# Mixture-of-experts stage: the products of two experts taken one after the other, with a semaphore for each expert's weights

## The reference

```python
def expert_block(args):
    xr, e = args
    return (jax.nn.silu(xr @ w_gate[e]) * (xr @ w_up[e])) @ w_down[e]
...
yb = lax.map(expert_block, (xb, blk_e)).reshape(cap, d)
return jnp.zeros_like(h).at[tok_buf].add(yb * w_buf[:, None])
```

## Time and profile before

| | us |
|---|---|
| median of 3 runs | 2017.88 (2017.27 to 2020.76) |
| profiled execution, its own time | 2020.66 |
| span of its profile | 2018.3 |
| PE busy | 1781.8 (88%), 7064 instructions |
| DVE, ACT, POOL busy | 729.9, 449.8, 397.5 |
| expert stage, first PE row to the last down products | 1475.67 to 1982.97 |
| mean granted TensorE clock | 0.955 |

### The profile page before, as it was taken

One profiled execution on the slowest core, in us unless ns is written; L12 is line 12 of the kernel. 1 busy time (PEld: TensorE's weight loads), 2 busy tenths in 40 slices (PEclk: granted clock), 3 DMA queues, 4 the chain that ended last, 5 costly groups with the idle time before them and its releaser, 6 DMA issues.

```text
span 2018.3 us, 18573 instructions
## 1 busy us (share of the span) xinstructions
PE 1781.8 (88%) x7064; PEld 963.0 (48%) x7064; DVE 729.9 (36%) x1148; ACT 449.8 (22%) x716; POOL 397.5 (20%) x464
## 2 busy tenths in 40 slices
PE   6899999999996999999999999998478878777782
PEld 1455555555554777677765444443423323333330
DVE  1534635455345665556665322124400000000003
ACT  2231231413224443434443000002110000000001
POOL 0103223141317443354441000000010000000000
PEclk9999999999998999999999999999589989899996
DMA  7212321322320111111132725212679999999993
GB/s 278 81 34 78 122 56 45 112 57 68 94 63 22 52 42 42 52 39 44 42 104 87 257 94 187 94 60 89 264 289 428 431 429 430 430 429 429 430 404 153
DMA packets 153554, 350.25 MB, mean 174 GB/s; under 512 B 14065, under 2 KB 104394, under 8 KB 140442
## 3 DMA queue, kind: packets, MB, share of 16 engines
q1 hardware_dynamic: 135962, 325.34, 42.8%
q10 hardware_dynamic: 12496, 15.75, 2.3%
q0 software_dynamic: 5040, 8.40, 1.1%
HBM read 346.09 MB, written 13.32 MB: 178 GB/s over the span
## 4 chain that ended last, share of the span: by engine, by line
PE 71%; DMA 19%; DVE 4%; POOL 3%; issue 2%; ACT 1%; SPq 0%; ACTq 0%; POOLq 0%; DVEq 0%
PE bank L498 10%; PE bank L709 10%; PE bank L747 6%; PE bank L2186 5%; PE bank L1702 5%; PE bank L1279 4%; PE bank L503 4%; DMA arena<-in_w_up_dram 3%; DMA stay<-in_w_up_dram 3%; DMA stay<-in_w_gate_dram 3%; PE bank L1704 3%; PE bank L1721 3%; PE bank L2204 3%; PE bank L494 3%; PE bank L1315 2%
## 5 line engine op out<-in xcount | busy, mean ns | idle before, releaser
L709 PE MATMUL bank<-stay,arena 128*128 128x512 f32 (+1 forms) x704 | 242.7, 501 | 9.9 <-DVE arena L934 7.7
L2186 PE MATMUL bank<-arena 128*64 128x512 f32 x832 | 201.3, 640 | 51.2 <-DMA arena<-in_w_up_dram 35.1
L709 PEld LDWEIGHTS bank<-stay,arena 128*128 128x128 f32 x704 | 133.5, 192 | 111.4 <-issue 101.3
L498 PE MATMUL bank<-arena 128*128 128x512 f32 x384 | 169.0, 593 | 1.5 <-ACT stay L610 1.5
L2186 PEld LDWEIGHTS bank<-arena 128*64 128x64 f32 x832 | 70.9, 147 | 180.1 <-issue 178.5
L2248 DVE TENSOR_TENSOR arena<-arena,bank 128x512 f32<-128x512 f32 x17 | 11.7, 688 | 325.8 <-PE bank L2186 325.8
L747 PE MATMUL bank<-arena,stay 128*128 128x512 f32 x256 | 114.0, 596 | 1.4 <-DVE arena L973 1.4
L1158 POOL TENSOR_TENSOR arena<-arena 128x256 f32<-128x256 f32 x112 | 86.6, 773 | 131.7 <-DVE arena L1472 117.5
L498 PEld LDWEIGHTS bank<-arena 128*128 128x128 f32 x384 | 71.7, 190 | 85.4 <-issue 85.4
L1471 DVE TENSOR_TENSOR arena<-arena 128x256 f32<-128x256 f32 x112 | 63.5, 607 | 132.0 <-ACT arena L1214 100.6
L2101 POOL DMA_INDIRECT y_dram<-arena x17 | 17.1, 1008 | 445.1 <-DVE arena L2255 444.5
(11 more groups left out here) (372 smaller groups left out, 2678.4 us busy)
## 6 DMA issues: line engine op xcount, KB each, us to landing
arena<-in_w_gate_dram SPq DMA_DIRECT2D x26, 2048.0 KB, 25.5
arena<-in_w_up_dram SPq DMA_DIRECT2D x26, 2048.0 KB, 26.9
arena<-in_w_down_dram SPq DMA_DIRECT2D x24, 2048.0 KB, 27.5
arena<-in_w_in_dram SPq DMA_DIRECT2D x58, 512.0 KB, 3.9
arena<-in_w_ada_dram SPq DMA_DIRECT2D x12, 2048.0 KB, 10.9
stay<-in_w_down_dram SPq DMA_DIRECT2D x10, 2048.0 KB, 26.0
stay<-in_w_gate_dram SPq DMA_DIRECT2D x8, 2048.0 KB, 25.7
stay<-in_w_up_dram SPq DMA_DIRECT2D x8, 2048.0 KB, 28.2
```

The lines of the kernel that those rows point to most:

```text
L498: mm = pe.matmul(b[:, :], w[:, k, :], src[:, k, 0:LAT], start=(k == 0), stop=(k == KT - 1))
L709: mm = pe.matmul(ps[:, 0:n], w[:, k, :], hT[:, k, o:o + n], start=(k == 0), stop=(k == KT - 1))
L2186: mm = pe.matmul(b[cols, :], xgT[r][:, k, cols], w[u][:, k, :], start=(k == 0), stop=(k == KT - 1))
```

## The change

The four semaphores `s_w` take only the loads of the first expert, and four other semaphores, which earlier stages had used (`s_x`, `s_ctx`, `s_wdt`, `s_ysum`, standing at 16, 16, 16 and 8), take the loads of the second. PE waits for the first expert's load, does all of its products of the group (16 instructions), waits for the second's and does all of its products. In `down` both output halves of the first expert come ahead of those of the second. What is computed, the loads, their order and the buffers are the same.

```diff
+        s_w_second = [s_x, s_ctx, s_wdt, s_ysum]
+        SECOND = [16, 16, 16, 8]
...
         def landed(chunk):
-            return 32 * (chunk // 4 + 1)
+            return 16 * (chunk // 4 + 1)
...
-                for u in range(2):
-                    sp.dma_start(weights_of(chunk)[u], expert_source(kind, pair[u])).then_inc(s_w[chunk % 4], 16)
+                sp.dma_start(weights_of(chunk)[0], expert_source(kind, pair[0])).then_inc(s_w[chunk % 4], 16)
+                sp.dma_start(weights_of(chunk)[1], expert_source(kind, pair[1])).then_inc(s_w_second[chunk % 4], 16)
...
             def up(chunk, r, loaded, b, done):
                 w = weights_of(chunk)
-                pe.wait_ge(s_w[chunk % 4], loaded)
-                for k in range(KT):
-                    for u in range(2):
-                        cols = slice(u * SLOT, (u + 1) * SLOT)
+                for u in range(2):
+                    if u:
+                        pe.wait_ge(s_w_second[chunk % 4], loaded + SECOND[chunk % 4])
+                    else:
+                        pe.wait_ge(s_w[chunk % 4], loaded)
+                    cols = slice(u * SLOT, (u + 1) * SLOT)
+                    for k in range(KT):
                         mm = pe.matmul(b[cols, :], xgT[r][:, k, cols], w[u][:, k, :], start=(k == 0), stop=(k == KT - 1))
                 mm.then_inc(done, 1)
...
             def down(chunk, loaded, done):
                 w = weights_of(chunk)
                 pe.wait_ge(s_guc, done + 1)
-                pe.wait_ge(s_w[chunk % 4], loaded)
-                for hf in range(2):
-                    for f in range(FT):
-                        for u in range(2):
-                            cols = slice(u * SLOT, (u + 1) * SLOT)
+                for u in range(2):
+                    if u:
+                        pe.wait_ge(s_w_second[chunk % 4], loaded + SECOND[chunk % 4])
+                    else:
+                        pe.wait_ge(s_w[chunk % 4], loaded)
+                    cols = slice(u * SLOT, (u + 1) * SLOT)
+                    for hf in range(2):
+                        for f in range(FT):
                             mm = pe.matmul(bank[5 + hf][cols, :], guT[:, f, cols], w[u][:, f, hf * 512:(hf + 1) * 512],
                                            start=(f == 0), stop=(f == FT - 1))
                 mm.then_inc(s_d, 1)
...
-                up(OVER, 0, landed(OVER) + i * 32, bank[2], s_g)
+                up(OVER, 0, landed(OVER) + i * 16, bank[2], s_g)
```

More of the change, by code:

```diff
@@ L2231, in experts_tensor @@
                 pe.wait_ge(s_sig, PAIRS + i)
-                up(OVER, 0, landed(OVER) + i * 32, bank[2], s_g)
+                up(OVER, 0, landed(OVER) + i * 16, bank[2], s_g)
                 pe.wait_ge(s_gu, PAIRS + i)
-                up(OVER + 1, 0, landed(OVER + 1) + i * 32, bank[3], s_u)
+                up(OVER + 1, 0, landed(OVER + 1) + i * 16, bank[3], s_u)
                 pe.wait_ge(s_guc, PAIRS + i)
@@ L2237, in experts_tensor @@
                 pe.wait_ge(s_yb, PAIRS + i)
-                down(OVER + 2, landed(OVER + 2) + i * 32, PAIRS + i)
+                down(OVER + 2, landed(OVER + 2) + i * 16, PAIRS + i)
         ylc = arena[:, 0:4096].rearrange("p (j d) -> p j d", d=D)
```

## The result

| | before | after |
|---|---|---|
| median of the runs, us | 2019.32 (2017.27 to 2021.93) | 2132.8 (2131.09 to 2134.19) |
| span of the profile, us | 2018.3 | 2129.6 |
| PE busy, us | 1781.8 | 1962.8 |
| mean granted TensorE clock | 0.955 | 0.97 |

The changed kernel is slower: ratio 1.0561, 95% interval 1.0543 to 1.0579, four runs of each in turn. Forecast were 2127.5 us, 2085 to 2203.

The account below looks back on a forecast made before the run. The weight-load queue bounds the expert stage at 30.75 us a block; the new order makes PE the bound at 35.63 us. Over fifteen blocks and the overflow block that adds 109.6 us: 2127.5 us, range 2085 to 2203.

Parts of the forecast that it names:

- The bound: Expert stage: now limited by the queue of weight loads, 30.75 us a block; after the change by PE, 35.63 us.
- Both halves at once: Expert products: the array's two column halves run together, 16 slots a group; one half alone goes no faster.
- S = 4: Slots gained at each change of half, as three waiting pairs are passed: four, 1.72 us; S from 3 to 5: 0.72.
- four slots: Expert products: a slot is the 0.429 us for a pair of instructions, one on each half; four are 1.72 us.
- 3.6 steps: At L1914, 32 short instructions took 3.21 us, not 3.60; the saving counted in start intervals of 0.107 us.
- Rival 1: Expert products: matmuls start in program order, one slot gained a change; 42.07 us a block, 2234 us; 0.09 with two slots.
- rival 2: Expert products: a change of half empties the array first, no slot gained; 44.21 us a block, 2270 us; chance 0.04.
- rival 3: Expert products: TensorE looks seven or more slots ahead, queue stays the bound, 2018 to 2021 us; no difference 0.06.
- The sum: Expert stage: block (96 - 5 S) slots + 3.03 = 35.63 us, fifteen blocks, then overflow block; +109.6 us in all.
- The other edits at nothing: Second semaphore, reused semaphores and three more PE waits a block: 2.5 us in all at most, taken as 0.
- Rival 4: New wait lets PE start before the second expert's load; at most some 5 us once, 2013 us; chance 0.02.
- What to look for: Profile after: gate issues about 35.6 us apart, DMA share near 0.85, some 370 GB/s, PE clock 1.00, hardly any weight waits.

## Why the prediction was right

**The bound.** The stage was bound by the queue and is now bound by PE. The kernel with half loads shows it: half the bytes, the same block.

**Both halves at once.** Right, from the earlier trace rows against each other. With the queue's limit away the old order needs 23.66 us a block, beside the 23.62 read in the earlier trace rows, and the new one 35.92.

**S = 4.** This was the step on which all hung, and it rested on one place of the trace with short instructions at half clock. It was right: three waiting instructions are passed here too, and the kernels with runs of 4 and 8 instructions, and with one change less, each gave the block that three passed and four slots make, within 0.1, 0.6 and 0.1 us. The rows of L1914 had shown 3.6 steps and not four; the 0.4 of a step that is missing is 0.04 us, near the 0.05 us found above, but that the two are the same is not shown. Counting instructions, not time, was an assumption; instructions of 25 columns (at 0.50) and of 512 (at 1.00) now show the same three. Rival 1, program order with its 42.07 us a block, and rival 2 with 44.21 fall with the 35.92; rival 3 needed seven slots.

**The sum.** Term by term: a block is 35.92 us in place of 35.63, which is 4.3 us over fifteen blocks; 0.25 of the 0.29 fits the 0.05 us for each of five changes that the sum lacked. The products began 2.2 us sooner than in the profile before (1476.54 to 1478.78), which no step foresaw: 0.7 us by a shorter wait for the gather (15.03 for 15.76), and 1.5 us that were there before the expert stage, in code that the change does not touch (1455.20 to 1456.70, L1914). In the overflow block down came 0.5 us sooner, since it no longer waits for its weights. Together +111.3 us of span, forecast +109.6. The 1.5 us are luck; the medians differ by 113.5 us, 3.9 more than forecast, and that is about the 4.3 of the blocks.

**The other edits at nothing.** Right for the semaphores and waits (ratio 0.9996). Rival 4's early start brought nothing in the order of the change, as said, since PE was late for every load. The prediction gave it 5 us at most in a stage bound by the queue; split in a way that keeps the halves busy, it brought 5.9 us (2020.99 to 2015.11), or 5.5 by the ratios, each to its own runs of before (0.9999 and 0.9972), part of it by the clock.

**What to look for.** Clock 1.00, no waits for weights, blocks of 35.9: as named. The DMA share was named too low, 0.85 for 0.91 measured; the 366 GB/s are the 370 named. The share counts the time of packets, which is not in proportion to the bytes: 1.01 stood beside 430 GB/s, 0.91 beside 366 and 0.52 beside 191.

## What to carry to other kernels

Where products use half of the array's columns, the instructions of the two halves must alternate closely: in this kernel four in a row cost nothing, eight 2.30 us a block, and sixteen, one expert after the other, took half as much again (35.92 us a block for 23.66). It shows in full only where it is more than what the queue leaves over (here 7 us a block). To start before all of a load is there, split the load so that both halves have work in each part. And look in the trace for another place that already does what a change will do: 32 short instructions of the routing told what 1632 long ones would do.

## What the runs showed of the hardware

- TensorE starts matmuls of one half of the columns ahead of up to three waiting ones of the other half: 29 down instructions, then gate's first (1550.33). The block lengths with runs of 4, 8 and 16 instructions (23.69, 25.96, 35.92 us) and the 3.21 us of L1914, at 25 columns and a clock of 0.50, fit the same three.
- Where a half takes over ahead of waiting instructions of the other, its first two instructions start 0.48 us apart, not 0.43 (1533.86 and 1534.34; 1550.33 and 1550.81). With runs of four instructions the block is 23.69 us with 24 changes, so not every change costs this.
- The granted clock can fall to 0.50 inside one group: eight instructions in a row for each half took 10.61 us in place of 8.94, with 0.50 granted from 1978 to 1980.
- Loads of 1 MB in place of 2 MB: 426 GB/s in place of 430 with the queue full, the same in each of the three kernels that have them.
- From the issue of the first gather to the first transpose: 11.2 us with a 4 MB chunk issued ahead of it (1464.50 to 1475.67; 10.4 in the changed kernel), 5.3 us with half of that (1462.22 to 1467.54), 3.7 us with none (1465.54 to 1469.19).
